# Where the softmax division of the second stack's attention is done: on the output, or on GpSimd ahead of the transposes

## The chip, the cores and the metric

The kernel runs on one core of a Trainium2 chip. A core has five engines with queues of their own: TensorE (PE; PEld is its weight load), VectorE (DVE), ScalarE (ACT), GpSimd (POOL) and SyncE (SP, here only DMA issue). They run side by side and are held together by semaphores alone. The metric is the device time of one execution in microseconds; below, "us" is that. The kernel before takes 3553.91 us, the median of 3 runs (3548.20 to 3556.32).

## The reference

Two transformer stacks of two layers each run one after the other on 512 positions of width 1024. The change touches only the attention of the second stack. There, 12 heads of 96 query/key and 64 value dimensions attend over 512 positions (plus 256 context positions as keys; in the first layer the 256 context positions are queries too, over themselves):

```python
def mla_attend(q_nope, q_rope, k_nope, k_rope, v):
    s = jnp.einsum('bqhd,bkhd->bhqk', q_nope, k_nope) + jnp.einsum('bqhr,bkr->bhqk', q_rope, k_rope)
    p = jax.nn.softmax(s.astype(jnp.float32) * SOFTMAX_SCALE, axis=-1).astype(v.dtype)
    return jnp.einsum('bhqk,bkhd->bqhd', p, v)
...
# in second_block, per layer:
att_l = blocked_attention(qn_l, qr_l, k_nope_all, k_rope_all, v_all)
four_l = fourier_mix(f_in, w_fourier[l], b_fourier[l])
mix_l = jnp.concatenate([four_l, att_l], axis=-1) @ w_out[l]
x = x + gt1 * mix_l
# then the gated feed-forward part; in layer 0 the same for the context
```

The division by the sum can be done on the probabilities p (128 queries x up to 768 keys, queries on the partitions) or after the product with v on the output (128 x 128, where the queries lie along the free axis).

## The kernel before, in words

Most of the time goes to large products, in which a weight slab (1 MB, 128 x 2048) is loaded by SP into one of two slots of `wst`, its upper part is cut off by ACT into `whi`, and the remainder `wst - whi` goes to `wlo`. For most slabs DVE computes the remainder, for 40 of them POOL (`split`, L684). Six of these 40 lie in the second stack, three for each layer's attention; ACT makes their `whi` in two halves (`next_group`, L1914) during pairs 0, 2 and 4.

The attention of the second stack is a hand-written software pipeline. The work is cut into **units**: one pair of heads for one block of 128 queries. Layer 0 has 6 pairs x 6 units (four units with 768 keys, then two with 256 keys, the context), layer 1 has 6 pairs x 4 units (768 keys); 60 units in all. In the text (l, p, n) is unit n of pair p in layer l. Each engine runs its own program over the units, written in this order for iteration u (`par` 0 and 1 are the two heads of the pair):

- PE: `logits(u+1, 0)` into PSUM; `turn(u, 0)`, four 128x128 transposes of the probabilities in `S2`; `logits(u+1, 1)`; `turn(u, 1)`; a "mid" projection for the next pair, if there is one; `turn(u, 2)`; `weighted(u-1)`, the product with the values, in PSUM bank 6; `denominators(u-1)`; an "end" projection, if there is one. The transposes share PSUM banks 4 and 5 in turn (`RING2`), projections of later pairs use bank 7.
- DVE: `maximum(u+1, 0)` (copies the logits from PSUM to `S2` and leaves the negated row maximum); `reciprocals(u)` of the two sums; `copy(u)`, the first transposed chunk to `PT2`; `maximum(u+1, 1)`; its share of the mid projection; `normalized(u-1)`, output times reciprocals; its share of the end projection.
- ACT: `exponential(u+1, 0)` in place in `S2`, with the row sum into `den2`; copy of chunk 1; mid projection; `exponential(u+1, 1)`; copy of chunk 2; `denominators(u-1)`; end projection.

The output lies with its queries along the free axis, so the reciprocals (one for each partition) have to be spread: PE's `denominators` (L1392) multiplies the broadcast reciprocals with the identity, ACT copies that to `Rs2` (L1942), and DVE multiplies (L2779). A pair's next projections stand at its first three units (`PROJECT_AT`): n = 0 K in mid and QA at the end, n = 1 KV and QB, n = 2 V and (layer 0) QC at the end. The later units of a pair, and all units of pair 5, carry none. PE's `weighted(u)` waits until `normalized(u-1)` has freed bank 6, and `maximum(u+1, par)` until the transposes of unit u-1 have freed `S2`.

Lines of the profile: L1348 logits, L1365 transposes, L1380 product with the values, L1392 spreading the reciprocals, L1316 to L1318 query projection, L2755 maximum, L2763 reciprocals, L2771 and L1934 copies of transposed chunks, L2779 normalisation, L1925 exponential (its second instruction, the accumulator read, delivers the sum), L1434 the first product after the attention.

Of the kernel before, what the change touches and what calls it, by code (L numbers as in the profile page):

```python
# [305 lines left out]
def turn_ring_2():  # L306

    at, copied, chunk, counts = {}, [], {}, {"ACT": 0, "DVE": 0}

    def place_(key, engine):  # L310
        at[key] = len(copied)
        counts[engine] += 1
        copied.append((engine, counts[engine]))

    for l in range(DEPTH):
        for u in range(len(UNITS2[l]) + 1):
            if u < len(UNITS2[l]):
                for c in range(blocks2(l, u) // 4):
                    chunk[l, u, c] = len(chunk)
                    place_(("T", l, u, c), "ACT" if c else "DVE")  # L320
            if u:
                place_(("R", l, u - 1), "ACT")
    return at, copied, chunk
# [57 lines left out]
def two_stacks(nc, io, out):  # L381
    m, s = Names(), Names()
    with ExitStack() as ctx:
# [110 lines left out]
        m.Rs2, at = place(nc, at, "Rs2", [P, 2, P])  # L494
# [110 lines left out]
        s.rden2_ready, s.o2_ready = sem("rden2_ready"), sem("o2_ready")  # L605

# [71 lines left out]
        @block.gpsimd  # L678
        def _(pool):
            def split(slab):  # L680

                pool.wait_ge(s.lo_ready, slab + 2)
                pool.wait_ge(s.hi_ready, slab + 3)
                nc.gpsimd.tensor_tensor(m.wlo[:, slab % 2, :], m.wst[:, slab % 2, :], m.whi[:, slab % 2, :].bitcast(F32),  # L684
                                        ALU.subtract).then_inc(s.lo_ready, 1)

            nc.gpsimd.memset(m.cs[:, :, :], 0.0).then_inc(s.cs_clear, 1)
            pool.drain()
            for l in range(DEPTH):
                for c in list(range(SL_A + 2, SL_ADA)) + [SL_MERGE, SL_MERGE + 1]:  # L690
                    if c != SL_B:
                        split(l * SLABS1 + c)
            for l in range(DEPTH):
                for c in (S2_HG + 2, S2_FOUR, S2_WOUT):
                    split(SLAB_BASE2 + l * SLABS2 + c)
            pool.drain()
# [3 lines left out]
        def _(pe):  # L700
# [512 lines left out]
            for l in range(DEPTH):  # L1213
# [144 lines left out]
                def turn(u, c):  # L1358

                    at = RING2["T", l, u, c]  # L1360
                    pe.wait_ge(s.exp2_ready, 2 * (unit0 + u + 1))
                    bank = ring_bank(at)
                    for b in range(4):
                        kb = 2 * c + b // 2
                        last = pe.transpose(ps[bank][:, b * P:(b + 1) * P],  # L1365
                                            m.S2[:, 2 * (u % 2) + b % 2, kb * P:(kb + 1) * P], ident)
                    last.then_inc(s.t2_done, 1)
# [18 lines left out]
                def denominators(u):  # L1386

                    pe.wait_ge(s.rden2_ready, unit0 + u + 1)
                    bank = ring_bank(RING2["R", l, u])
                    for par in range(2):  # L1390
                        c = 2 * (u % 4) + par
                        last = pe.matmul(ps[bank][VH * par:VH * (par + 1), 0:P],  # L1392
                                         m.rden2[:, c:c + 1].broadcast_to([P, VH]), ident, start=True, stop=True)
                    last.then_inc(s.t2_done, 1)

# [5 lines left out]
                for u in range(len(units) + 1):  # L1401
# [15 lines left out]
                    if u:  # L1417
                        weighted(u - 1)
                        denominators(u - 1)
                    if here["end"] is not None:  # L1420
                        project(p + 1, here["end"])
                copied2(pe, RING2["R", l, len(units) - 1])
# [131 lines left out]
        def _(act):  # L1554
# [261 lines left out]
            for l in range(DEPTH):  # L1816
# [101 lines left out]
                def exponential(u, par):  # L1918

                    w, unit = blocks2(l, u) // 2 * P, unit0 + u  # L1920
                    if unit >= 4:
                        act.wait_ge(s.rden2_ready, unit - 3)
# [12 lines left out]

                def denominators(u):

                    at, unit = RING2["R", l, u], unit0 + u
                    act.wait_ge(s.t2_done, at + 1)
                    if unit >= 2:  # L1940
                        act.wait_ge(s.o2_ready, unit - 1)
                    act.activation(m.Rs2[:, u % 2, :], ps[4 + at % 2][:, 0:P], ACT.Copy).then_inc(s.t2_act, 1)  # L1942
# [5 lines left out]
                for u in range(len(units) + 1):  # L1948
# [13 lines left out]
                    if u:  # L1962
                        denominators(u - 1)
# [85 lines left out]
        def _(dve):  # L2049
# [543 lines left out]
            for l in range(DEPTH):  # L2593
# [165 lines left out]
                def reciprocals(u):  # L2759

                    dve.wait_ge(s.exp2_ready, 2 * (unit0 + u + 1))
                    c = 2 * (u % 4)
                    nc.vector.reciprocal(m.rden2[:, c:c + 2], m.den2[:, c:c + 2]).then_inc(s.rden2_ready, 1)  # L2763
# [9 lines left out]
                def normalized(u):  # L2773
# [4 lines left out]
                    copied2(dve, RING2["R", l, u])  # L2778
                    TT(m.OT2[:, p, c0:c0 + P], ps[6][:, 0:P], m.Rs2[:, u % 2, :], ALU.mult).then_inc(s.o2_ready, 1)  # L2779
# [3 lines left out]
                for par in range(2):  # L2783
                    maximum(0, par)
                for u in range(len(units) + 1):
# [5 lines left out]
                    if u < len(units):  # L2791
                        reciprocals(u)
                        copy(u)
                    if u + 1 < len(units):
                        maximum(u + 1, 1)
                    if here["mid"] is not None:
                        projected(p + 1, here["mid"])
                    if u:
                        normalized(u - 1)
                    if here["end"] is not None:  # L2800
# [243 lines left out]
```

## Time and profile before

| what | value |
|---|---|
| median of 3 runs | 3553.91 us (3548.20 to 3556.32) |
| profiled execution | 3557.09 us, span 3555.3 us |
| PE busy / PEld busy | 3448.0 us (97%) / 2802.5 us (79%) |
| DVE busy | 2086.4 us (59%) |
| ACT busy | 1348.5 us (38%) |
| POOL busy | 187.9 us (5%), 45 instructions |
| chain that ended last | PE 83%, DVE 9%, ACT 4% |
| attention stretches of the second stack | about 1945 to 2174 and 2915 to 3100 us |

Times of the trace count from the start of the span. A timeline row gives the start and the duration of an instruction, or of several alike run together (x4), its engine and line, what it writes and reads, and in brackets how long the engine had been idle and what ended that. The busy figure of PE is modelled from pipelined instructions, so distances between starts of the weight loads (PEld) tell the pace more exactly.

### The profile page before, as it was taken

What the parts mean: (1) busy time and instruction counts of PE and PEld (TensorE: products, weight loads), DVE (VectorE), ACT (ScalarE), POOL (GpSimd) and SP (SyncE); (2) the same over time, 40 slices, a digit from 0 to 9 for tenths busy, and PEclk for the clock granted to TensorE, in tenths of its full rate; (3) what the DMA queues carried; (4) which work ended last, traced back from release to release, by engine and by line L of the source; (5) the groups of instructions that cost most, each with busy time, mean ns of one, the idle gap of its engine ahead of it and who ended that gap; (6) DMA issues with size and microseconds to landing.
All of it is one profiled execution on the core that took longest, in us unless ns stands there. A gap on an engine that the chain in (4) does not pass through costs nothing.

```text
span 3555.3 us, 53450 instructions
## 1 busy us (share of the span) xinstructions
PE 3448.0 (97%) x20094; PEld 2802.5 (79%) x20094; DVE 2086.4 (59%) x3313; ACT 1348.5 (38%) x2115; POOL 187.9 (5%) x45
## 2 busy tenths in 40 slices
PE   7999999999999999999998999999999989999998
PEld 6766888888777678888888776888888877688887
DVE  7876457444677745645566654653544665456546
ACT  5546333222453643322213554241323235534322
POOL 2321000000133010000000000000000001000000
PEclk9999999999999999999999999999999999999999
DMA  3235232222222633322221001111111110112222
GB/s 141 76 140 212 107 119 104 96 95 94 83 95 84 239 121 115 128 95 95 95 95 48 13 13 56 48 71 60 60 71 60 60 72 25 44 61 106 95 95 83
DMA packets 45639, 317.27 MB, mean 89 GB/s; under 512 B 4992, under 2 KB 7296, under 8 KB 8192
## 3 DMA queue, kind: packets, MB, share of 16 engines
q1 hardware_dynamic: 44720, 307.11, 23.4%
q10 hardware_dynamic: 720, 7.40, 0.5%
q8 instruction: 138, 2.26, 0.2%
q14 instruction: 61, 0.50, 0.0%
HBM read 312.39 MB, written 2.10 MB: 88 GB/s over the span
## 4 chain that ended last, share of the span: by engine, by line
PE 83%; DVE 9%; ACT 4%; DVEq 2%; issue 2%; POOL 0%; DMA 0%; ACTq 0%; SPq 0%; POOLq 0%
PE psum L722 21%; PE psum L726 21%; PE psum L723 21%; PE psum L1348 4%; PE psum L1380 2%; PE psum L1365 2%; DVE MA L2309 1%; PE psum L806 1%; PE psum L1183 1%; PE psum L1443 1%; PE psum L869 1%; ACT whi L1560 1%; ACT xs L1570 1%; PE psum L1316 1%; DVE BQK L2073 1%
## 5 line engine op out<-in xcount | busy, mean ns | idle before, releaser
L722 PE MATMUL psum<-xh,whi 128*128 128x512 f32 (+1 forms) x2224 | 857.6, 388 | 3.9 <-DVE xc L2064 2.1
L723 PE MATMUL psum<-xl,whi 128*128 128x512 f32 (+1 forms) x2224 | 850.9, 385 | 0.0
L1560 ACT ACTIVATE whi<-wst 128x2048 fp32r<-128x2048 f32 x234 | 447.0, 1910 | 582.9 <-PE psum L726 553.6
L2055 DVE TENSOR_TENSOR wlo<-wst,whi 128x2048 fp32r<-128x2048 f32 x200 | 458.2, 2291 | 176.8 <-ACT whi L1560 175.4
L726 PE MATMUL psum<-xh,wlo 128*128 128x512 f32 (+1 forms) x2224 | 536.5, 383 | 0.2
L722 PEld LDWEIGHTS psum<-xh,whi 128*128 128x128 f32 x2224 | 420.2, 189 | 97.3 <-issue 15.7
L723 PEld LDWEIGHTS psum<-xl,whi 128*128 128x128 f32 x2224 | 420.0, 189 | 82.4 <-issue 1.2
L726 PEld LDWEIGHTS psum<-xh,wlo 128*128 128x128 f32 x2224 | 409.7, 188 | 82.7 <-POOL wlo L684 1.1
L684 POOL TENSOR_TENSOR wlo<-wst,whi 128x2048 fp32r<-128x2048 f32 x40 | 187.2, 4680 | 2888.6 <-ACT whi L1914 1779.0
L722 PE MATMUL psum<-uh,whi 128*128 128x512 f32 x480 | 189.8, 395 | 0.0
L723 PE MATMUL psum<-ul,whi 128*128 128x512 f32 x480 | 189.5, 395 | 0.0
L722 PE MATMUL psum<-gh,whi 128*128 128x512 f32 (+1 forms) x576 | 188.3, 344 | 0.8 <-DVE gl L2906 0.8
L723 PE MATMUL psum<-gl,whi 128*128 128x512 f32 (+1 forms) x576 | 187.5, 343 | 0.0
L1348 PE MATMUL psum<-K,Q 96*128 96x256 f32 (+1 forms) x432 | 158.3, 486 | 1.4 <-DVE Q L2740 1.2
L1925 ACT ACTIVATE S<-S,nmax 128x768 f32<-128x768 f32 (+1 forms) x120 | 101.8, 848 | 127.2 <-DVE rden L2763 110.7
L1794 ACT ACTIVATE uh<-ur 128x512 f32 x64 | 40.5, 633 | 250.8 <-DVE ur L2553 250.8
L2573 DVE TENSOR_TENSOR hT<-hT,psum 128x512 f32<-128x512 f32 x64 | 44.0, 687 | 145.7 <-PE psum L726 126.3
L2839 DVE SCALAR_TENSOR_TENSOR hT<-psum,mod,hT 128x512 f32<-128x512 f32 (+1 forms) x80 | 51.3, 643 | 125.4 <-PE psum L726 125.4
L726 PE MATMUL psum<-uh,wlo 128*128 128x512 f32 x480 | 122.5, 395 | 0.0
L722 PE MATMUL psum<-xch,whi 128*128 128x256 f32 x488 | 121.3, 287 | 0.0
L722 PEld LDWEIGHTS psum<-gh,whi 128*128 128x128 f32 x576 | 109.4, 190 | 15.0 <-DVE gl L2906 1.2
L723 PE MATMUL psum<-xcl,whi 128*128 128x256 f32 x488 | 120.6, 286 | 0.0
(364 smaller groups left out, 5731.2 us busy)
## 6 DMA issues: line engine op xcount, KB each, us to landing
wst<-weights SPq DMA_DIRECT2D x288, 1024.0 KB, 4.8
dft<-c_dft ACTq DMA_DIRECT2D x2, 2688.0 KB, 10.5
hT<-x_t SPq DMA_DIRECT2D x4, 512.0 KB, 7.7
cT<-ctx_t ACTq DMA_DIRECT2D x1, 1024.0 KB, 6.9
out<-hT SPq DMA_DIRECT2D x1, 1024.0 KB, 5.4
out<-hT SPq DMA_DIRECT2D x2, 512.0 KB, 4.3
masks<-c_masks SPq DMA_DIRECT2D x1, 644.0 KB, 11.5
ropes<-c_ropes ACTq DMA_DIRECT2D x1, 512.0 KB, 7.6
```

Source lines behind the costliest of these rows:

```text
L684: nc.gpsimd.tensor_tensor(m.wlo[:, slab % 2, :], m.wst[:, slab % 2, :], m.whi[:, slab % 2, :].bitcast(F32), ALU.subtract).then_inc(s.lo_re ...
L722: pe.matmul(out, weights(m.whi, k), head(k), start=opens and n == 0, stop=False)
L723: pe.matmul(out, weights(m.whi, k), tail(k), start=False, stop=False)
L726: last = pe.matmul(out, weights(m.wlo, k), head(k), start=False, stop=closes and k == list(kts)[-1])
L1348: last = pe.matmul(ps[2 * par + c // 512][:, 0:w], m.Q4[0:QH, at, q0:q0 + P], m.K4[0:QH, at, side * T + c:side * T + c + w], start=True, s ...
L1365: last = pe.transpose(ps[bank][:, b * P:(b + 1) * P], m.S2[:, 2 * (u % 2) + b % 2, kb * P:(kb + 1) * P], ident)
L1380: mm = pe.matmul(ps[6][VH * par:VH * (par + 1), 0:P], m.V4[:, 4 * side + b // 2, col:col + VH], m.PT2[:, CHUNK2[l, u, c] % 5, (b % 4) * P: ...
L1560: act.activation(m.whi[:, slot, :], m.wst[:, slot, :], ACT.Copy).then_inc(s.hi_ready, 1)
L1925: act.activation(sc, sc, ACT.Exp, bias=m.nmax2[:, 2 * (u % 2) + par:2 * (u % 2) + par + 1], scale=-1.0, accum_out=m.den2[:, c:c + 1]).then ...
L2055: TT(m.wlo[:, slot, :], m.wst[:, slot, :], m.whi[:, slot, :].bitcast(F32), ALU.subtract).then_inc(s.lo_ready, 1)
L2573: TT(h, h, ps[(FR_MLP + j) % 4][:, :], ALU.add).then_inc(s.acc_free, 1)
L2839: STT(h, ps[t % 4][:, 0:n], g, h, ALU.mult, ALU.add).then_inc(s.acc_free, 1)
```

## The change

- `denominators` goes on both PE and ACT, with `Rs2` and the ring entries "R". The ring of PSUM banks 4 and 5 holds transposes alone.
- DVE's `reciprocals(u)` for both heads becomes `reciprocal(u, par)` for each. `reciprocal(u+1, 0)` stands after `copy(u)` and ahead of `maximum(u+1, 1)`; `reciprocal(u+1, 1)` stands after `normalized(u-1)`. For the first unit of a layer both stand ahead of the loop.
- POOL multiplies each head's probabilities in `S2`, in place, with the reciprocal, and signals `p2_normed`. PE's transposes wait for that instead of the exponential.
- DVE's `normalized` becomes a plain copy of bank 6.
- POOL's six weight remainders of the second stack (128x2048) are cut into four pieces of 128x512 each, one behind each of the first four units of pairs 1, 3 and 5.

```diff
+            def split_part(slab, n):
+                cols = slice(n * SLAB // 4, (n + 1) * SLAB // 4)
+                if n == 0:
+                    pool.wait_ge(s.lo_ready, slab + 2)
+                    pool.wait_ge(s.hi_ready, slab + 3)
+                ins = nc.gpsimd.tensor_tensor(m.wlo[:, slab % 2, cols], m.wst[:, slab % 2, cols],
+                                              m.whi[:, slab % 2, cols].bitcast(F32), ALU.subtract)
+                if n == 3:
+                    pool.drain()
+                    pool.sem_inc(s.lo_ready, 1)
+
             for l in range(DEPTH):
-                for c in (S2_HG + 2, S2_FOUR, S2_WOUT):
-                    split(SLAB_BASE2 + l * SLABS2 + c)
+                for u in range(len(UNITS2[l])):
+                    unit, w = UNIT2[l] + u, blocks2(l, u) // 2 * P
+                    for par in range(2):
+                        pool.wait_ge(s.rden2_ready, 2 * unit + par + 1)
+                        sc, c = m.S2[:, 2 * (u % 2) + par, 0:w], 2 * (u % 4) + par
+                        nc.gpsimd.tensor_scalar(sc, sc, m.rden2[:, c:c + 1], None, ALU.mult).then_inc(s.p2_normed, 1)
+                    p, n = divmod(u, len(SIDES2[l]))
+                    if p % 2 and n < 4:
+                        split_part(SLAB_BASE2 + l * SLABS2 + S2_HG + p // 2 + 2, n)
...
                 def turn(u, c):
-                    pe.wait_ge(s.exp2_ready, 2 * (unit0 + u + 1))
+                    pe.wait_ge(s.p2_normed, 2 * (unit0 + u + 1))
...
-                def denominators(u):
-
-                    pe.wait_ge(s.rden2_ready, unit0 + u + 1)
-                    bank = ring_bank(RING2["R", l, u])
-                    for par in range(2):
-                        c = 2 * (u % 4) + par
-                        last = pe.matmul(ps[bank][VH * par:VH * (par + 1), 0:P],
-                                         m.rden2[:, c:c + 1].broadcast_to([P, VH]), ident, start=True, stop=True)
-                    last.then_inc(s.t2_done, 1)
...
-                def reciprocals(u):
-
-                    dve.wait_ge(s.exp2_ready, 2 * (unit0 + u + 1))
-                    c = 2 * (u % 4)
-                    nc.vector.reciprocal(m.rden2[:, c:c + 2], m.den2[:, c:c + 2]).then_inc(s.rden2_ready, 1)
+                def reciprocal(u, par):
+
+                    dve.wait_ge(s.exp2_ready, 2 * (unit0 + u) + par + 1)
+                    c = 2 * (u % 4) + par
+                    nc.vector.reciprocal(m.rden2[:, c:c + 1], m.den2[:, c:c + 1]).then_inc(s.rden2_ready, 1)
...
-                    copied2(dve, RING2["R", l, u])
-                    TT(m.OT2[:, p, c0:c0 + P], ps[6][:, 0:P], m.Rs2[:, u % 2, :], ALU.mult).then_inc(s.o2_ready, 1)
+                    nc.vector.tensor_copy(m.OT2[:, p, c0:c0 + P], ps[6][:, 0:P]).then_inc(s.o2_ready, 1)
```

DVE's queue in the last pair of layer 1, before. ISA is the maximum with its accumulator read, `PT_138` the transposed chunk, `OT_126` the output, `Rs_139` the spread reciprocals:

```order
L2755 ISA S_137,nmax_144<-psum,none 128x768 [waits l2_done,t2_done]
L2755 ISA nmax_144 128x1
L2763 RECIPROCAL rden_143<-den_142 128x2 [waits exp2_ready]
L2771 COPY PT_138<-psum 128x512 [waits pv2_done,t2_done]
L2755 ISA S_137,nmax_144<-psum,none 128x768 [waits l2_done,t2_done]
L2755 ISA nmax_144 128x1
L2779 TENSOR_TENSOR OT_126<-psum,Rs_139 128x128 [waits t2_act,pv2_done]
```

The same stretch of DVE's queue in the changed kernel:

```order
L2749 ISA S_137,nmax_143<-psum,none 128x768 [waits l2_done,t2_done]
L2749 ISA nmax_143 128x1
L2765 COPY PT_138<-psum 128x512 [waits pv2_done,t2_done]
L2757 RECIPROCAL rden_142<-den_141 128x1 [waits exp2_ready]
L2749 ISA S_137,nmax_143<-psum,none 128x768 [waits l2_done,t2_done]
L2749 ISA nmax_143 128x1
L2772 COPY OT_126<-psum 128x128 [waits pv2_done]
L2757 RECIPROCAL rden_142<-den_141 128x1 [waits exp2_ready]
```

The second maximum now stands behind a reciprocal that waits for the first head's exponential of the same unit, and the second reciprocal stands behind the copy of the output, which waits for the product with the values.

PE's queue in the same pair, before, from the end of one unit's product with the values to the next unit's transposes (64x128 rows are halves of the output, 128x512 and 128x256 the logits):

```order
L1380 MATMUL psum<-PT_138,V_152 64x128 x3
L1392 MATMUL psum<-cst,rden_143 64x128 [waits t2_act,rden2_ready]
L1392 MATMUL psum<-cst,rden_143 64x128
L1348 MATMUL psum<-K_151,Q_150 128x512 [waits p2_act,p2_dve,max2_ready]
L1348 MATMUL psum<-K_151,Q_150 128x256
L1365 MATMUL psum<-cst,S_137 128x128 [waits t2_act,exp2_ready]
L1365 MATMUL psum<-cst,S_137 128x128 x3
```

And in the changed kernel:

```order
L1396 MATMUL psum<-PT_138,V_151 64x128 x3
L1364 MATMUL psum<-K_150,Q_149 128x512 [waits p2_act,p2_dve,max2_ready]
L1364 MATMUL psum<-K_150,Q_149 128x256
L1381 MATMUL psum<-cst,S_137 128x128 [waits t2_act,p2_normed]
L1381 MATMUL psum<-cst,S_137 128x128 x3
```

The two products with the reciprocals are gone, and the transposes wait for POOL's signal; nothing else in PE's order moves.

## Rows read from the trace of the kernel before

**Rows 1.** Windows, the two attention stretches: busy time and instructions of each engine, PEclk, DMA.

```profile
1945.00:2174.00 229.00, 222.48 (x1731) 168.93 (x1730) 130.01 (x312) 120.43 (x278) 13.57 (x3) 1.00 0.07 27
2915.00:3100.00 185.00, 180.66 (x1374) 136.32 (x1374) 99.15 (x214) 102.97 (x214) 13.67 (x3) 0.99 0.09 33
```

**Rows 2.** Timeline, second layer, one unit without projections, (1,5,1) to (1,5,2).

```profile
3077.95 0.58 PEld L1365 LDWEIGHTS psum<-cst,S 128*128 128x128 f32 x4
3078.47 0.96 DVE L2755 CUSTOM_DVE_ANT_0 S<-psum,none 128x768 f32<-128x768 f32 x1 [0.91 <-PE psum L1348]
3079.53 0.94 ACT L1925 ACTIVATE S<-S,nmax 128x768 f32<-128x768 f32 x1 [2.36 <-DVE rden L2763]
3080.20 0.96 DVE L2755 CUSTOM_DVE_ANT_0 S<-psum,none 128x768 f32<-128x768 f32 x1
3080.86 1.53 PE L1380 MATMUL psum<-PT,V 128*64 128x128 f32 x24
3082.11 0.19 ACT L1925 ACTIVATION_READ_ACCUMULATOR S<-S,nmax 128x1 f32 x1
3082.12 0.25 PEld L1392 LDWEIGHTS psum<-cst,rden 128*64 128x64 f32 x4
3082.54 0.30 PEld L1348 LDWEIGHTS psum<-K,Q 96*128 96x128 f32 x2 [0.17 <-issue]
3083.05 0.29 DVE L2779 TENSOR_TENSOR OT<-psum,Rs 128x128 f32<-128x128 f32 x1 [1.87 <-ACT Rs L1942]
3083.72 0.58 PEld L1365 LDWEIGHTS psum<-cst,S 128*128 128x128 f32 x4
```

**Rows 3.** Timeline, last short unit of a pair to the next pair's first, (0,3,5) to (0,4,0).

```profile
2101.49 0.58 PEld L1365 LDWEIGHTS psum<-cst,S 128*128 128x128 f32 x4
2102.02 0.96 DVE L2755 CUSTOM_DVE_ANT_0 S<-psum,none 128x768 f32<-128x768 f32 x1 [0.92 <-PE psum L1348]
2103.75 0.96 DVE L2755 CUSTOM_DVE_ANT_0 S<-psum,none 128x768 f32<-128x768 f32 x1
2105.65 0.19 ACT L1925 ACTIVATION_READ_ACCUMULATOR S<-S,nmax 128x1 f32 x1
2105.89 0.42 PEld L1365 LDWEIGHTS psum<-cst,S 128*128 128x128 f32 x4 [0.40 <-ACT S L1925]
```

**Rows 4.** Timeline of PE, layer 0, the end of the iteration before (0,4,4).

```profile
2134.27 0.39 PE L1380 MATMUL psum<-PT,V 128*64 128x128 f32 x4
2134.81 0.70 PE L1348 MATMUL psum<-K,Q 96*128 96x256 f32 x2
2135.34 0.60 PE L1365 MATMUL psum<-cst,S 128*128 128x128 f32 x4
```

**Rows 5.** Timeline, a unit reached behind two projections, (1,1,1).

```profile
2955.57 0.19 ACT L1925 ACTIVATION_READ_ACCUMULATOR S<-S,nmax 128x1 f32 x1
2959.53 0.58 PEld L1365 LDWEIGHTS psum<-cst,S 128*128 128x128 f32 x4
```

**Rows 6.** Groups of instructions: count, busy us, mean ns, idle before.

```profile
L684 POOL TENSOR_TENSOR wlo<-wst,whi 128x2048 fp32r<-128x2048 f32 x40 | 187.2, 4680 | 2888.6 <-ACT whi L1914 1779.0 <-ACT whi L1560 1109.2
L687 POOL MEMSET cs<- 128x512 f32 x1 | 0.5, 524 | 0.3 <-POOLq L3036 0.3
L1392 PEld LDWEIGHTS psum<-cst,rden 128*64 128x64 f32 x240 | 15.2, 137 | 0.0
L2763 DVE RECIPROCAL rden<-den 128x2 f32<-128x2 f32 x60 | 9.6, 159 | 0.0
```

**Rows 7.** Timeline, ACT's half of a weight slab and POOL's start behind it.

```profile
1981.63 1.05 ACT L1914 ACTIVATE whi<-wst 128x1024 fp32r<-128x1024 f32 x1
1982.82 4.52 POOL L684 TENSOR_TENSOR wlo<-wst,whi 128x2048 fp32r<-128x2048 f32 x1 [712.05 <-ACT whi L1914]
```

**Rows 8.** Timeline, the end of layer 1's attention.

```profile
3094.53 0.25 PEld L1392 LDWEIGHTS psum<-cst,rden 128*64 128x64 f32 x4
3095.45 0.29 DVE L2779 TENSOR_TENSOR OT<-psum,Rs 128x128 f32<-128x128 f32 x1 [2.23 <-ACT Rs L1942]
3095.81 0.73 PEld L1434 LDWEIGHTS psum<-dft,fT 128*128 128x128 f32 x4 [1.03 <-ACT Rs L1942]
```

**Rows 9.** Timeline, an idle time of PE with the clock kept.

```profile
1944.50 0.30 PE L1334 MATMUL psum<-whi,ckvh 128*128 128x128 f32 x1 [2.35 <-ACT K L1897]
```

More of the change, by code:

```diff
@@ L315, in turn_ring_2 @@
     for l in range(DEPTH):
[L316 to L322, printed above, removed]
+        for u in range(len(UNITS2[l])):
+            for c in range(blocks2(l, u) // 4):
+                chunk[l, u, c] = len(chunk)
+                place_(("T", l, u, c), "ACT" if c else "DVE")
     return at, copied, chunk
@@ L493, in two_stacks @@
         m.PT2, at = place(nc, at, "PT2", [P, 5, 4 * P])
-        m.Rs2, at = place(nc, at, "Rs2", [P, 2, P])
         m.none, at = place(nc, at, "none", [P, 1])
@@ L605, in two_stacks @@
         s.rden2_ready, s.o2_ready = sem("rden2_ready"), sem("o2_ready")
+        s.p2_normed = sem("p2_normed")
         s.oth_ready, s.mixed = sem("oth_ready"), sem("mixed")
@@ L692, in _ @@
                         split(l * SLABS1 + c)
-            for l in range(DEPTH):
-                for c in (S2_HG + 2, S2_FOUR, S2_WOUT):
-                    split(SLAB_BASE2 + l * SLABS2 + c)
+            def split_part(slab, n):
[8 more added lines that the diff above has]
+                    pool.sem_inc(s.lo_ready, 1)
+            for l in range(DEPTH):
+                for u in range(len(UNITS2[l])):
+                    unit, w = UNIT2[l] + u, blocks2(l, u) // 2 * P
[6 more added lines that the diff above has]
+                        split_part(SLAB_BASE2 + l * SLABS2 + S2_HG + p // 2 + 2, n)
             pool.drain()
@@ L1418, in _ @@
                         weighted(u - 1)
-                        denominators(u - 1)
                     if here["end"] is not None:
                         project(p + 1, here["end"])
-                copied2(pe, RING2["R", l, len(units) - 1])
                 pe.wait_ge(s.o2_ready, unit0 + len(units))
@@ L1921, in exponential @@
                     if unit >= 4:
-                        act.wait_ge(s.rden2_ready, unit - 3)
+                        act.wait_ge(s.p2_normed, 2 * (unit - 3))
                     act.wait_ge(s.max2_ready, 2 * unit + par + 1)
@@ L1934, in copy @@
                     act.activation(m.PT2[:, chunk % 5, :], ps[4 + at % 2][:, :], ACT.Copy).then_inc(s.t2_act, 1)
[L1936 to L1942, printed above, removed]
                 for n in range(len(PROJECTED[l])):
@@ L1961, in _ @@
                         copy(u, 2)
-                    if u:
-                        denominators(u - 1)
                     if here["end"] is not None:
@@ L2784, in _ @@
                     maximum(0, par)
+                for par in range(2):
+                    reciprocal(0, par)
                 for u in range(len(units) + 1):
@@ L2791, in _ @@
                     if u < len(units):
-                        reciprocals(u)
                         copy(u)
                     if u + 1 < len(units):
+                        reciprocal(u + 1, 0)
                         maximum(u + 1, 1)
@@ L2799, in _ @@
                         normalized(u - 1)
+                    if u + 1 < len(units):
+                        reciprocal(u + 1, 1)
                     if here["end"] is not None:
```

## The prediction

> **What bounds the kernel now.** I read the page first: PE is busy almost all the time, and the chain that ended last runs mostly through it. So a change counts if it takes work from PE or makes PE wait. The two stretches that the change touches come next [rows 1]: PE is busy for 222.5 of 229 us and 180.7 of 185 us, while DVE, ACT and POOL have room. POOL works for 13.6 us in each, three weight remainders. PE is the bound here, but only just: the softmax of a unit has to be done before PE comes to its transposes.
>
> So the third reading was the timeline, unit by unit. For each of the 60 units I compared the end of its second exponential with the start of the first transposes. The reader should see three kinds of unit. Behind a projection the probabilities are ready long before PE wants them: in (1,1,1) at 2955.76, and PE comes at 2959.53, 3.8 us later [rows 5]. Without projections 1.4 us are left: ready at 3082.30, wanted at 3083.72 [rows 2]. From a pair's last short unit to the next pair nothing is left: ready at 2105.84, PE starts at 2105.89 after an idle time of 0.40 us [rows 3]. The change puts two more steps between the exponential and the transposes, a reciprocal and a POOL instruction. What matters is in how many units they fit.
>
> **What goes.** The products with the reciprocals: 240 weight loads, 15.2 us busy [rows 6], so 0.25 us for each of 60 units. That is PE time, on the path wherever PE doesn't wait. ACT's copy to `Rs2` and the wait of DVE for it were hidden (1.87 us idle before the normalisation at 3083.05, and nobody waited for DVE there [rows 2]); their end only matters at a layer's end. The ring without its "R" entries lets a transpose wait for an earlier copy than before, worth nothing where the copies are in time.
>
> **What is added.** From the end of the second exponential to the transposes there was one wake-up, 0.05 us [rows 3]. Now: wake DVE 0.05, reciprocal 0.16 (159 ns for two sums, taken for one too [rows 6]), wake POOL 0.14 (ACT ends at 1982.68, POOL starts at 1982.82 [rows 7]), POOL's multiply T, wake PE 0.05. That is T + 0.40 us.
>
> T isn't in the trace. From below, a memset of 512 elements takes 524 ns, 1.02 ns an element, and only writes; the multiply also reads, so I don't go under 0.79 us for 768 elements and 0.26 for 256. From above, the remainder reads two tensors: 4.52 us for 2048 [rows 7], 2.21 ns an element, so 1.70 and 0.57 us. With one tensor read I stay nearer to the memset: 1.3 ns an element, T = 1.0 us, and 0.4 us for the short units.
>
> The Trainium skill (GPSIMD Engine Reference, Engine selection) advises against GpSimd for elementwise work, though it calls one-input operations roughly line-rate; the trace agrees with the two-input half of that, 4.52 us on POOL where the page gives 4497 ns. Its section Elementwise, side-by-side cycle accounting, has 769 ns for 512 elements in a tight loop. By that, as an estimate, T would be 1.15 us and the sum below 15 us; no row here shows it.
>
> Two orders on DVE cost more than the instructions. First, the second maximum now waits for the first head's exponential. In [rows 3] the first maximum starts at 2102.02. From the start of a maximum to the end of its exponential are 2.09 us (2103.75 to 2105.84). So that exponential ends at 2104.11, the reciprocal at 2104.32, and the second maximum starts there and not at 2103.75: 0.57 us later. Second, the second reciprocal stands behind the copy of the output, which waits for the product with the values.
>
> **The sum by kinds of transition**, from one unit's first transposes to the next unit's (58 of them):
>
> A. Last short unit to next pair, 5 times, layer 0. The exponential ends 0.57 later, at 2106.41; plus T + 0.40 gives 2107.81 against 2105.89. That is 1.92 each, 9.6 us.
>
> B. Full units without an end projection, 13 times. The product with the values ends at 3080.86 + 1.53 = 3082.39 [rows 2]. Then wake 0.05, copy 0.29 (as the normalisation), reciprocal 0.16, wake 0.14, T, wake 0.05: 3084.08 against 3083.72. The exponential would end at 3082.30 + 0.57 = 3082.87 in the first such unit, 0.14 behind the copy; once PE has waited, the first maximum starts earlier relative to PE and that goes. A group that waited runs through in 0.42 and not 0.58 us [rows 3], since its weight load no longer stands behind logits, which gives back 0.16. So 0.20 each, 2.6 us.
>
> C. Short logits in between, 6 times in layer 0. Product with the values ends at 2134.66 [rows 4]; plus 0.69 and 0.4 is 2135.75 against 2135.34, and 0.05 for the group's run: 0.45 each, 2.7 us.
>
> D. Four transitions in the last pairs, worked in the same way: 0.65 for (0,5,0) to (0,5,1), 1.07, 0.95, and 1.2 for the last of layer 1, where no logits follow the product. 3.9 us.
>
> E. The other 30, behind projections or with enough logits in between: all of it hides, and the 0.25 comes off. The slack is 3.8 us in [rows 5] against 0.6 + 1.4 + 0.25. Minus 7.5 us.
>
> F. Ends. A layer's first unit waits T + 0.35 more, 1.35 twice: 2.7 us. At a layer's end, before, the next product starts at 3095.81, behind products, ACT's copy and the normalisation [rows 8]; now the copy follows the product at once, 0.6 earlier, for each of the last two units: 4 x 0.6, minus 2.4 us.
>
> The quarters of weight remainders take about 1.15 us each (a quarter of 4.52) and start when PE starts transposing; POOL's next multiply comes over 2 us later, so they cost nothing. Without that cover a multiply would be late by what is left of a quarter. Their slabs are wanted two or more pairs later, or behind the Fourier part; SP's next load starts later by the time of the four units, and DMA's share in these stretches is 0.07 to 0.09 [rows 1].
>
> Sum: 9.6 + 2.6 + 2.7 + 3.9 - 7.5 + 2.7 - 2.4 = +11.6 us. The profiled execution took 3557.1 us, 3 us over the median of the runs; on the median the forecast is 3553.9 + 11.6 = 3565.5 us. T counts in 23 places in full and in 7 for the short units. At the lower bound the sum is 11.6 - 0.21 x 23 - 0.14 x 7 = +5.8, at the upper 11.6 + 0.70 x 23 + 0.17 x 7 = +28.9.
>
> **Rivals.**
> 1. POOL at the pace of the memset: 3553.9 + 5.8 = 3559.7 us, no change that can be told (about 0.2%, 7 us, is what a measurement tells here; that bound holds for the chances below). For it: only one tensor is read. Against it: a memset reads nothing.
> 2. POOL at the pace of the remainder: 3553.9 + 28.9 = 3582.8 us. For it: the only arithmetic that POOL shows runs so. Against it: half the reading.
> 3. Faster. PE hides the new steps nearly everywhere, because engines run ahead: when PE has waited once, the next unit's first maximum starts earlier relative to PE, so the order on DVE stops costing (0.57 of A goes too) and T is short. It needs T under 0.64 us, from where B turns into a gain (3083.08 + T against 3083.72). Then B to E give back up to 0.25 each: the full price is 15.2 + 2.4 = 17.6 us, 3536 us; with A still paid, 3545. Against it: the memset alone gives 0.79.
> 4. The clock. In A, PE idles for about 2.6 us five times. One idle time of 2.35 us [rows 9] lies at the edge of a stretch with PEclk 1.00 [rows 1], so I expect no fall. If each brought what layer 1's stretch lost (0.99 over 185 us, 1.9 us), 9 us more: 3575 us.
>
> **How the numbers follow.** Forecast 0.50 (own range 3561 to 3573), rival 1 0.20, rival 2 0.14, rival 3 0.09, rival 4 0.07. The range takes in rivals 1, 2 and 4 and the bounds of T, with 3 us for the spread of the runs: 3556 to 3584. Faster: rival 3, 0.08. Within 0.2%: rival 1 and the low edge of the forecast, 0.20. Slower: 0.72.
>
> **What would show it.** POOL's multiply has a row: its mean for 768 elements is T. PE's transposes should wait for POOL for about 2.6 us at 5 places in layer 0 and for about 0.5 us in units without projections; the stretch of layer 0 grows by about 10 us and that of layer 1 by about 1. Units behind projections should be 0.25 us shorter. The forecast is wrong if T is under 0.64 us, if DVE's second maximum doesn't start later in A, or if PE's clock falls in the idle times.

## The result and the profile after

The changed kernel takes 3620.43 us (median of 4 runs, 3617.52 to 3621.04) against 3553.94 us: a ratio of 1.0185, 95% interval 1.0172 to 1.0199. The forecast of 3565.5 us and its range up to 3584 are both missed; the direction was right. The profiled execution took 3617.5 us with a span of 3615.7 us. It was the shortest of the four, and that of the kernel before, 3557.1 us, was longer than the median: the two profiles are 60.4 us apart, the medians 66.5.

Groups of instructions on POOL between 1930 and 3200 us, one for each shape. These answer to [rows 6]:

```profile
L708 POOL TENSOR_SCALAR S<-S,rden 128x768 f32<-128x768 f32 x96 | 212.3, 2212 | 1584.3 <-DVE rden L2757 1583.8
L696 POOL TENSOR_TENSOR wlo<-wst,whi 128x512 fp32r<-128x512 f32 x24 | 30.6, 1275 | 0.0
L708 POOL TENSOR_SCALAR S<-S,rden 128x256 f32<-128x256 f32 x24 | 23.4, 975 | 31.8 <-DVE rden L2757 31.8
```

T is 2.21 us for 768 columns and 0.975 us for 256. The upper bound of the prediction, 1.70 and 0.57 us, was no bound.

The windows of the two stretches, [rows 1] before (columns: PE, PEld, DVE, ACT, POOL busy, then PEclk, DMA share, GB/s). The attention of layer 0 now runs on to about 2210, that of layer 1 from about 2957 to 3157:

```profile
1945.00:2174.00 229.00, 201.19 (x1355) 146.48 (x1353) 121.63 (x301) 95.58 (x202) 122.16 (x70) 0.93 0.03 10
2915.00:3100.00 185.00, 165.18 (x1095) 125.80 (x1096) 103.89 (x212) 83.40 (x156) 86.97 (x43) 0.96 0.10 34
```

PE is no longer busy throughout, and the granted clock has fallen from 1.00 to 0.93 in the first. The timeline of a full unit without projections, (1,5,0) to (1,5,1), for [rows 2]:

```profile
3127.99 0.42 PEld L1381 LDWEIGHTS psum<-cst,S 128*128 128x128 f32 x4 [1.70 <-POOL S L708]
3129.54 2.20 POOL L708 TENSOR_SCALAR S<-S,rden 128x768 f32<-128x768 f32 x1 [0.37 <-DVE rden L2757]
3130.09 0.96 DVE L2749 CUSTOM_DVE_ANT_0 S<-psum,none 128x768 f32<-128x768 f32 x1 [0.64 <-PE psum L1364]
3131.99 0.19 ACT L1929 ACTIVATION_READ_ACCUMULATOR S<-S,nmax 128x1 f32 x1
3132.35 0.29 DVE L2772 COPY OT<-psum 128x128 f32<-128x128 f32 x1 [1.30 <-PE psum L1396]
3132.56 0.15 DVE L2757 RECIPROCAL rden<-den 128x1 f32<-128x1 f32 x1
3132.80 2.20 POOL L708 TENSOR_SCALAR S<-S,rden 128x768 f32<-128x768 f32 x1 [1.06 <-DVE rden L2757]
3134.97 1.28 POOL L696 TENSOR_TENSOR wlo<-wst,whi 128x512 fp32r<-128x512 f32 x1
3135.06 0.42 PEld L1381 LDWEIGHTS psum<-cst,S 128*128 128x128 f32 x4 [1.70 <-POOL S L708]
```

The unit takes 7.07 us where it took 5.77. The order is as the prediction read it: copy of the output, reciprocal, multiply, transposes, each waiting for the one before. The quarter of a weight remainder (1.28 us) starts with the transposes and is done before the next multiply. From a short unit to the next pair, (0,3,5) to (0,4,0), for [rows 3]:

```profile
2125.59 0.42 PEld L1381 LDWEIGHTS psum<-cst,S 128*128 128x128 f32 x4 [0.42 <-POOL S L708]
2125.72 0.96 DVE L2749 CUSTOM_DVE_ANT_0 S<-psum,none 128x768 f32<-128x768 f32 x1 [1.20 <-PE psum L1364]
2127.96 0.96 DVE L2749 CUSTOM_DVE_ANT_0 S<-psum,none 128x768 f32<-128x768 f32 x1
2128.10 4.44 POOL L708 TENSOR_SCALAR S<-S,rden 128x768 f32<-128x768 f32 x2 [2.56 <-DVE rden L2757]
2129.86 0.19 ACT L1929 ACTIVATION_READ_ACCUMULATOR S<-S,nmax 128x1 f32 x1
2132.59 0.60 PEld L1381 LDWEIGHTS psum<-cst,S 128*128 128x128 f32 x4 [3.38 <-POOL S L708]
2133.39 2.77 PE L1364 MATMUL psum<-K,Q 96*128 96x512 f32 x4
```

7.00 us where it was 4.40. Here POOL itself is the chain: its two multiplies stand one behind the other (x2, 4.44 us). And behind this wait (3.38 us between weight loads, 2.98 us between PE's own products) PE runs at half speed: logits that take 1.46 us elsewhere take 2.77.

Two more rows answer to [rows 5] and [rows 8]. A unit behind two projections, (1,1,1), has its exponential ready 3.6 us early and doesn't wait:

```profile
3002.65 0.19 ACT L1929 ACTIVATION_READ_ACCUMULATOR S<-S,nmax 128x1 f32 x1
3006.40 0.58 PEld L1381 LDWEIGHTS psum<-cst,S 128*128 128x128 f32 x4
```

At the end of layer 1 the next product's weight load starts 0.66 us behind the last load of the values' product. Before, it was 1.28 us: the loads for the reciprocals, 0.25, and an idle time of 1.03 [rows 8].

```profile
3154.46 1.29 PEld L1396 LDWEIGHTS psum<-PT,V 128*64 128x64 f32 x24 [0.67 <-DVE OT L2772]
3156.07 0.29 DVE L2772 COPY OT<-psum 128x128 f32<-128x128 f32 x1 [1.66 <-PE psum L1396]
3156.41 0.73 PEld L1438 LDWEIGHTS psum<-dft,fT 128*128 128x128 f32 x4 [0.66 <-DVE OT L2772]
```

### The profile page after: what moved, and what is told of

It reads as the page before. It is cut to its first block, busy times and chain, and to the rows that moved or that the text cites. A ratio compares the mean times of both kernels' runs of the same rounds, so it can differ in the third digit from the quotient of the medians.

```text
span 3615.7 us, 52934 instructions
## 1 busy us (share of the span) xinstructions
PE 3458.5 (96%) x19854; PEld 2797.9 (77%) x19854; DVE 2099.6 (58%) x3373; ACT 1335.4 (37%) x2055; POOL 426.1 (12%) x183
## 3 DMA queue, kind: packets, MB, share of 16 engines
q8 instruction: 135, 2.21, 0.3%
## 4 chain that ended last, share of the span: by engine, by line
PE 80%; DVE 9%; ACT 4%; POOL 2%; issue 2%; DVEq 2%; DMA 0%; POOLq 0%; ACTq 0%; SPq 0%
PE psum L738 20%; PE psum L742 20%; PE psum L739 20%; PE psum L1364 3%; PE psum L1381 2%; POOL S L708 2%; PE psum L1396 2%; DVE MA L2303 1%; PE psum L822 1%; PE psum L1199 1%; PE psum L1447 1%; PE psum L885 1%; ACT whi L1564 1%; ACT xs L1574 1%; PE psum L1332 1%
## 5 line engine op out<-in xcount | busy, mean ns | idle before, releaser
L708 POOL TENSOR_SCALAR S<-S,rden 128x768 f32<-128x768 f32 (+1 forms) x120 | 235.7, 1964 | 1616.1 <-DVE rden L2757 1615.6
L681 POOL TENSOR_TENSOR wlo<-wst,whi 128x2048 fp32r<-128x2048 f32 x34 | 159.9, 4704 | 1107.6 <-ACT whi L1564 1107.3
L1364 PE MATMUL psum<-K,Q 96*128 96x256 f32 (+1 forms) x432 | 168.0, 511 | 1.2 <-DVE Q L2734 1.2
L1381 PE MATMUL psum<-cst,S 128*128 128x128 f32 x624 | 103.1, 295 | 58.5 <-POOL S L708 55.6
L1381 PEld LDWEIGHTS psum<-cst,S 128*128 128x128 f32 x624 | 78.8, 151 | 85.9 <-POOL S L708 71.5
L2749 DVE CUSTOM_DVE_ANT_0 S<-psum,none 128x768 f32<-128x768 f32 (+1 forms) x120 | 101.9, 849 | 51.0 <-PE psum L1364 49.9
L1364 PEld LDWEIGHTS psum<-K,Q 96*128 96x128 f32 x432 | 79.1, 201 | 59.5 <-issue 57.2
```

The source lines that it names most:

```text
L708: nc.gpsimd.tensor_scalar(sc, sc, m.rden2[:, c:c + 1], None, ALU.mult).then_inc(s.p2_normed, 1)
L1364: last = pe.matmul(ps[2 * par + c // 512][:, 0:w], m.Q4[0:QH, at, q0:q0 + P], m.K4[0:QH, at, side * T + c:side * T + c + w], start=True, s ...
L1381: last = pe.transpose(ps[bank][:, b * P:(b + 1) * P], m.S2[:, 2 * (u % 2) + b % 2, kb * P:(kb + 1) * P], ident)
L2749: nc.vector.tensor_tensor_reduce(m.S2[:, at, 0:w], psum[:, 1024 * par:1024 * par + w], m.none[:, 0:1].broadcast_to([P, w]), -1.0, -TAKEN, ...
```

## The experiments

Medians of before differ a little between the groups of runs (3552.7 to 3554.6 us); ratios are against those of the same group.

**The length of the multiply.** Two kernels change only the number of columns that it works on.

```diff
-   sc, c = m.S2[:, 2 * (u % 2) + par, 0:w], 2 * (u % 4) + par
+   sc, c = m.S2[:, 2 * (u % 2) + par, 0:64], 2 * (u % 4) + par        # e1_short
+   sc, c = m.S2[:, 2 * (u % 2) + par, 0:w // 2], 2 * (u % 4) + par    # e1_half
```

> The changed kernel with POOL's multiply cut to 64 columns a head (the rest of the probabilities is left undivided, so the output isn't the reference's); every wait and every order stays. Theory (the length of the multiply is what costs): the changed kernel shows 2.2 us for 768 columns and about 0.95 for 256, so some 0.5 us for 64. With T = 0.5 the prediction's own sum gives 11.6 - 0.5 x 23 + 0.1 x 7 = about +1 us against before, 3550 to 3560 us, and PE's clock doesn't fall in the attention. Rival (the extra hop and the order on DVE cost by themselves): at least 20 us over before, 3575 us or more.

Measured: 3558.15 us, ratio 1.0007 (0.9998 to 1.0016). The multiply took 460 ns. All hops, waits and orders of the change are in this kernel, and it costs 3.6 us by the medians, with an interval that takes in no change at all. The clock fell a little after all (0.98 and 0.99 in the two windows): three units behind a wait of PE took 1.6 to 1.7 us more than the same units of e5_warm below, in which PE keeps full speed there. The rival is out: of 66 us nearly all hangs on T, the waits and PE's slow stretches behind them together.

> The changed kernel with POOL's multiply over half the columns of each head (384 or 128; the other half is left undivided, so the output isn't the reference's). From the rows of 64, 256 and 768 columns (0.47, 0.975, 2.21 us) T should be about 1.3 and 0.65 us. Theory (time follows T): the prediction's sum with these gives 11.6 + 0.3 x 23 + 0.25 x 7 = +20 us, and less of the clock's fall than in the changed kernel: 3572 to 3590 us. Rival (a threshold, below which it is all hidden): 3560 us or less.

Measured: 3580.72 us, ratio 1.0066 (1.0046 to 1.0087), T = 1.25 us. The rival of a threshold is out too: 0.46, 1.25 and 2.21 us give +4, +26 and +66 us. The clock had already fallen here, to 0.94 and 0.96 in the two windows. A wait of PE for POOL, and the logits behind it, at (0,2,0):

```profile
2038.21 1.12 PE L1381 MATMUL psum<-cst,S 128*128 128x128 f32 x4 [2.34 <-POOL S L708]
2039.12 2.77 PE L1364 MATMUL psum<-K,Q 96*128 96x512 f32 x4
```

In six units (the first of each layer and of pairs 1 to 4 of layer 0) PE waited 2.3 to 2.6 us, and these took 1.6 to 2.9 us more than in e5_warm, 13.2 us together, half of the 26.

**What makes T.**

```diff
-   nc.gpsimd.tensor_scalar(sc, sc, m.rden2[:, c:c + 1], None, ALU.mult)
+   nc.gpsimd.tensor_scalar(sc, sc, 0.5, None, ALU.mult)                                       # e9_imm
+   nc.gpsimd.tensor_tensor(sc, sc, m.rden2[:, c:c + 1].broadcast_to([P, w]), ALU.mult)        # e10_tt
```

> The changed kernel with POOL multiplying by the constant 0.5 in place of the reciprocals (the output isn't the reference's). If the 2.21 us for 768 columns come from the multiplier that is read for each partition, the row should be clearly shorter, 1.0 to 1.5 us; if they are what this instruction costs on POOL whatever the multiplier, it stays at 2.2 us and the time at 3620 us.

> The changed kernel with POOL's multiply written as a product of two tensors, the second the reciprocal broadcast along the row. At the rate of the weight remainders (4.53 us for 2048 columns, 1.27 to 1.28 for 512, so 1.1 us for each 512 and 0.2 beside) 768 columns take about 1.8 us, 0.4 less than now: the two-input form would be the faster one, and the time falls by 0.4 x 23 = 9 us to about 3611 us. Rival (a two-input form is slower than one with a scalar, as the prediction took for granted): 3620 us or more.

POOL's rows of the two, e9_imm first:

```profile
L708 POOL TENSOR_SCALAR S<-S 128x768 f32<-128x768 f32 x96 | 205.2, 2138 | 1590.6 <-DVE rden L2757 1590.2
```

```profile
L708 POOL TENSOR_TENSOR S<-S,rden 128x768 f32<-128x768 f32 x96 | 141.5, 1475 | 1630.9 <-DVE rden L2757 1630.9
L708 POOL TENSOR_TENSOR S<-S,rden 128x256 f32<-128x256 f32 x24 | 16.0, 666 | 36.4 <-DVE rden L2757 36.4
```

With a constant it is 2.14 us, so the multiplier that is read for each partition isn't the reason (a single run: 3612.7 us). As a product of two tensors the same arithmetic takes 1.475 us, 3591.15 us in all, ratio 1.0105 (1.0088 to 1.0122): 29 us less than the changed kernel with one line written in another way. I had expected 9.

**The clock.**

```diff
+                def keep_busy(u):      # PE, called ahead of turn(u, 0)
+                    ...                # count: 8 at a layer's first unit, 6 or 3 in layer 0 as told below
+                    for _ in range(count):
+                        pe.matmul(ps[7][:, 0:256], ident, m.cst[:, 0:256], start=True, stop=True)
```

> The changed kernel with products of the identity with constants into PSUM bank 7 put ahead of those first transposes that wait longest for POOL (8 of 128x256 at each layer's first unit, 6 at the first unit of pairs 1 to 5 of layer 0, 3 at the other units of its pair 5; about 0.43 us each, so less than the wait they stand in). Nothing else is changed. Theory (PE's clock falls behind these idle times and its slow stretches are part of the cost): the granted clock of 1945 to 2174 rises from 0.93 to 0.98 or more and the time falls by 8 to 20 us, 3600 to 3612 us. Rival (the slow stretches lie in waiting anyway): 3617 to 3623 us.

Measured: 3602.77 us, ratio 1.0140 (1.0125 to 1.0156), 17.7 us under the changed kernel. T is unchanged at 2212 ns. The granted clock of layer 0 is back at 1.00 (the changed kernel has 0.93 and, from 2174 to 2220, 0.89), and behind the filled wait the logits take 1.46 us again:

```profile
1945.00:2174.00 229.00, 214.45 (x1488) 160.20 (x1489) 128.75 (x314) 103.32 (x217) 129.16 (x74) 1.00 0.05 18
2174.00:2220.00 46.00, 43.24 (x247) 26.59 (x245) 14.23 (x41) 15.55 (x39) 15.76 (x11) 1.00 0.16 62
```

```profile
2123.04 2.75 PE L1395 MATMUL psum<-cst 128*128 128x256 f32 x12
2126.18 0.66 PE L1381 MATMUL psum<-cst,S 128*128 128x128 f32 x4 [0.39 <-POOL S L708]
2126.68 1.46 PE L1364 MATMUL psum<-K,Q 96*128 96x512 f32 x4
```

The passage to the new pair still takes 7.00 us; what got shorter is the unit behind it, from 9.0 to 10.4 us to 7.3. So the slow stretches are a second cost that the waits bring with them, 17.7 of the 66.5 us.

**The order on DVE, alone and in company.** e3_order is the kernel before with the reciprocals at their new places; e8_maxfirst is the changed kernel with one pair of lines exchanged.

```diff
-                        reciprocals(u)          # e3_order, in the kernel before
                         copy(u)
                     if u + 1 < len(units):
+                        reciprocal(u + 1, 0)
                         maximum(u + 1, 1)
...
                         normalized(u - 1)
+                    if u + 1 < len(units):
+                        reciprocal(u + 1, 1)
...
-                        reciprocal(u + 1, 0)    # e8_maxfirst, in the changed kernel
                         maximum(u + 1, 1)
+                        reciprocal(u + 1, 0)
```

> The kernel before with nothing but the new places of the reciprocals on DVE: one for each head, the first ahead of the second maximum. Products with the reciprocals, ACT's copy and the whole weight remainders stay. The prediction's term: the second maximum 0.57 us later, paid at the 5 passages from a short unit to the next pair, +2.9 us, and 1 us for the rest: 3557 to 3559 us. Rival (the order holds up every unit without a projection too): +10 us or more.

> The changed kernel with DVE's second maximum ahead of the first head's reciprocal. Theory (POOL's two multiplies stand one behind the other and the first reciprocal starts that chain): the first multiply starts about 0.9 us later, the second with it, in all units in which PE waits for POOL, about 20 of them: 3632 to 3642 us. Rival (the later second maximum is what costs, as the prediction's term of 0.57 us says): 3608 to 3616 us.

e3_order: 3562.76 us, ratio 1.0022 (1.0012 to 1.0031), +8 us, twice what I gave it. The passages to the next pair cost 0.5 to 0.7 us each, 2.9 together, as reckoned (4.39 to 4.90 us in three of them). Two places had been put down as hidden. DVE's K copy stands behind the later second maximum, and PE needs it before the end projection: the first units of pairs 1 to 4 of layer 0 are 1.9 us longer together. And three transitions in the last pairs are 0.5 to 0.6 us longer each. In the profiles this makes 5.8 of the 8 us; the rest is not told apart. The K copy in unit (0,2,0), where PE waits 1.02 us in e3_order and 0.26 before:

```profile
2033.55 0.96 DVE L2755 CUSTOM_DVE_ANT_0 S<-psum,none 128x768 f32<-128x768 f32 x1
2034.55 0.69 DVE L2734 COPY K<-psum 64x512 f32<-64x512 f32 x1
2035.30 0.19 PEld L1316 LDWEIGHTS psum<-cqh,whi 128*128 128x128 f32 x1 [1.02 <-DVE K L2734]
```

e8_maxfirst: 3637.00 us, ratio 1.0234 (1.0218 to 1.0250). With a long T, putting the maximum ahead of the waiting reciprocal costs 17 us more, since POOL's chain of two multiplies starts with that reciprocal. Some of it is slow clock again: two units of layer 1 went from 8.19 to 9.9 us, with logits of 2.77 us. The reciprocal first is a loss without POOL's multiply and right with it.

**The quarters.**

```diff
-                    if p % 2 and n < 4:
-                        split_part(SLAB_BASE2 + l * SLABS2 + S2_HG + p // 2 + 2, n)
+                    if p % 2 and n == 0:
+                        split(SLAB_BASE2 + l * SLABS2 + S2_HG + p // 2 + 2)
```

> The changed kernel with POOL's weight remainders of the second stack whole again, 128x2048 in one piece behind the first unit of pairs 1, 3 and 5. Theory (a whole piece of 4.5 us stands ahead of the next unit's multiplies): it starts when PE starts transposing and ends at +4.6, the two multiplies of 2.2 us end at +9.0 where the second unit's transposes now come at +8.2 to +9.0, so up to 0.9 us six times: 3622 to 3626 us. Rival (POOL's queue has room for it, the quarters bring nothing): 3618 to 3621 us.

Measured: 3620.54 us, ratio 1.0189 (1.0173 to 1.0205), as the rival had it. Yet the mechanism of the theory is there: in layer 1 the units behind a whole piece take 8.89 us and not 8.19, and 8.87 and 8.74 in the last pair for 7.07; the layer is 5.2 us longer, 0.6 of it slow clock at its start. Layer 0 got 4.6 us shorter. 2.6 us of that lie in units in which PE's slow stretches fell differently, such as (0,5,3) to (0,5,4) with 5.13 for 6.39. Another 1.8 us lie in pair 1, where PE is at full speed in both kernels, and show a price of the quarters. The changed kernel there, then e6_whole:

```profile
2026.31 1.39 POOL L696 TENSOR_TENSOR wlo<-wst,whi 128x512 fp32r<-128x512 f32 x1
2026.43 1.82 DVE L2801 SCALAR_TENSOR_TENSOR hT<-hT,sm,r 128x512 f32<-128x512 f32 x1
2029.34 0.63 PE L1381 MATMUL psum<-cst,S 128*128 128x128 f32 x4 [1.42 <-DVE PT L2765]
```

```profile
2025.50 0.74 DVE L2801 SCALAR_TENSOR_TENSOR hT<-hT,sm,r 128x512 f32<-128x512 f32 x1
```

A DVE instruction of this stretch (an update of `hT` that has nothing to do with attention) takes 1.82 us beside a quarter and 0.74 without one; PE then waits 1.42 us for DVE's copy behind it, and 0.33 in e6_whole. So the quarters are worth some 4.5 us in layer 1 and cost 1.8 in layer 0; with the slow clock falling otherwise, the total shows neither.

**What could be won.**

```diff
-                    pe.wait_ge(s.p2_normed, 2 * (unit0 + u + 1))     # e2_nodiv; POOL's multiplies are left out
+                    pe.wait_ge(s.exp2_ready, 2 * (unit0 + u + 1))
...
+                def divided(u, par):      # e4_dve, on DVE behind maximum(u, 1) and the mid projection
+                    dve.wait_ge(s.exp2_ready, 2 * (unit0 + u) + par + 1)
...
+                    nc.vector.reciprocal(m.rden2[:, c:c + 1], m.den2[:, c:c + 1])
+                    dve.drain()
+                    TS(sc, sc, m.rden2[:, c:c + 1], None, ALU.mult).then_inc(s.p2_normed, 1)
```

> The changed kernel without any division (POOL's multiplies are left out, PE's transposes wait for the exponentials as before; the output isn't divided by the sums). It is the gain that the change could have at most. By the prediction's terms: 15.2 us of products on PE and 2.4 at the layers' ends, 3554 - 17.6 = 3536 us, plus 3 us for the order on DVE that stays = 3539. Rival (PE's saved time is taken back by waits for bank 7 and for the exponentials): 3548 us or more.

> The changed kernel with the multiply on DVE in place of POOL (reciprocal, drain, multiply in place, for each head behind the second maximum and the mid projection). If DVE needs 0.4 to 0.8 us for 768 columns (a DVE pass over 512 columns from PSUM takes 0.69 us in the trace, from SBUF it may be shorter), most units have the slack, DVE stays under 85% in the stretches, and PE keeps most of its 17.6 us: 3540 to 3548 us, faster than both kernels. Rival (DVE becomes the bound, since it is behind in the units with both a K copy and a rotation): 3554 to 3565 us.

e2_nodiv: 3542.03 us, ratio 0.9963 (0.9949 to 0.9976), 12.5 us less than before where I expected 15; e3_order shows that the order on DVE costs more than the 3 us taken for it. e4_dve: 3553.82 us, ratio 0.9998 (0.9989 to 1.0007), neither faster nor slower, where 3540 to 3548 us were expected. A multiply takes 0.62 us there, and layer 1 keeps its gain (5.55 for 5.77 us, 8.64 for 8.86, 6.87 for 7.09), but the passages in layer 0 pay it back (5.1 to 5.3 us for 4.40), and both layers start with a stretch of slow clock.

That led to e7_hybrid: the multiply on DVE where there is time, the old way where there is none.

```diff
+def is_spread(l, u):      # these units keep products, ring entry, Rs2 and normalisation of the kernel before
+    p, n = divmod(u, len(SIDES2[l]))
+    return n == 0 and (l == 0 or p == 0) or l == 0 and (n == 5 and p % 2 == 0 or p == 5 and n in (1, 3, 5)) or (l, p, n) == (1, 5, 3)
```

> A version meant to beat both. The multiply is on DVE (as in e4_dve) for the units that have time between exponential and transposes; the old way, products that spread the reciprocals and the transposes right behind the exponential, stays for 13 units: the first of each layer, the first of layer 0's later pairs, the last short ones of pairs 0, 2 and 4 and 4 in the last pairs. Against e4_dve (3554 us): 5 x 1.0 at the first units, 3 x 0.7 at the short ones, 3 at the starts of the layers, 1 in the last pairs: 3542 to 3546 us. Rival (mixing the two ways costs what it saves): 3552 us or more.

Measured: 3544.13 us, ratio 0.9970 (0.9959 to 0.9981). It beats both kernels, by 0.30% and by 2.1%. The passages are at 4.40 us again, the units behind them at 7.3 to 7.5. The old way stays for 14 of the 60 units (the expectation counts 13). Not all of the gain need be the division's: the first passage took 5.78 us in the kernel before, where DVE's update of `hT` took 2.67 us beside POOL's whole remainder. It takes 4.40 here, where POOL works in quarters and the update beside them takes 0.76. No run changes that alone.

## Why the prediction was wrong

Its frame held: which units have time, what follows what, and that the change makes the kernel slower. One term was mis-sized, T; one cost was put at nothing, the fall of PE's clock; and some waits that were put down as hidden were not.

**T, the step that failed.** "From above, the remainder reads two tensors: ... so 1.70 and 0.57 us." I took a two-input instruction for an upper bound of a one-input one. The scalar form costs 2.4 ns an element (2.21 and 0.975 us for 768 and 256) and even the product of tensors with a broadcast second input costs less. The Trainium skill calls one-input operations on GpSimd roughly line-rate (GPSIMD Engine Reference, Engine selection); neither this nor the 1.15 us estimated from its tight loop agrees with this trace, and the measurement decides. Its advice against elementwise work there is borne out: DVE needs 0.62 us for the same product. With the measured T the prediction's own sum is 11.6 + 1.21 x 23 + 0.575 x 7 = 43.5 us, beyond its range already. By kinds of transition, from the two profiles (the slow clock is what e5_warm takes off the same transitions):

| kind | forecast at T = 1.0 | the same at the measured T | measured | of which slow clock |
|---|---|---|---|---|
| A, 5 | +9.6 | +15.7 | +12.3 | |
| B, 13 | +2.6 | +18.3 | +17.7 | |
| C, 6 | +2.7 | +6.2 | +6.9 | 1.2 |
| D, 4 | +3.9 | +8.1 | +9.6 | 2.0 |
| E, 30 | -7.5 | -7.5 | +12.2 | 14.2 |
| F, starts and ends | +0.3 | +2.7 | +5.6 | 1.2 |
| sum | +11.6 | +43.5 | +64.3 | 18.6 |

B is the term that T carries: 1.30 us each in eight of the thirteen and 1.46 in the five behind a V projection, for which 0.20 + 1.21 = 1.41 follows from the forecast's working. A came out lower than 1.92 + 1.21 = 3.13 each: 2.6 to 3.0 in four of the five. In the rows of (0,3,5) DVE's second maximum did start 0.5 us later (2.24 us behind the first, 1.73 before), but it no longer counted: POOL's two multiplies in a row became the chain. The first passage grew by 1.4 us only, since it had been 5.78 us before, with PE waiting for a DVE that was held up beside POOL's whole remainder.

**Rival 4, the clock, given 0.07.** It happened, and not as a rival but on top: 17.7 us by the medians. The prediction judged from one idle time of 2.35 us without a fall and reckoned with 2.6 us of idling. With T = 2.21 PE itself waited 3.0 to 3.3 us at the passages and 4.3 at a layer's first unit, and behind these waits it ran at the lower of its two levels, 1.2 in place of 2.4 GHz. Nor would a shorter T have saved the step: in e1_half PE waited 2.3 to 2.6 us, as the prediction reckoned, and was slow behind all six of these waits. One idle time without a fall was no ground for expecting none. The slow clock is why E, "all of it hides", is at +12.2: it makes 14.2 us. Without them E is at -2.0.

**E, the rest.** Where nothing waited, the 0.25 us came off as forecast, or more (8.64 for 8.86 us in layer 1, 8.19 for 8.58). Not so at the fourth unit of layer 0's pairs, 8.54 for 8.37, where PE's weight load waited 0.43 us for POOL: with T = 1.25 it is 8.14. Nor between the two short units of a pair, 4.06 to 4.48 us for 4.04, which makes 2.2 us against the forecast. The units (0,1,1) and (0,1,2) add 1.3 us. e6_whole takes 0.7 off these two, and 1.1 off (0,1,3) in C, where DVE no longer stands beside a quarter: of the quarters, "they cost nothing" was wrong there.

**The order on DVE** was priced at 2.9 us, and at its place correctly; e3_order shows 8 by itself, since the K copy behind the maximum and the last pairs had been overlooked.

**F.** A layer's first unit waits 4.69 and 4.77 us and not 1.19 and 1.29: 3.5 more, not 1.35, being T and, again, two multiplies in a row. At a layer's end the step from the last values' product on gained 0.62 for the 0.6 us reckoned. From the last unit's transposes on, layer 0 gained 1.4 us, and layer 1 nothing (7.21 us for 7.15), as PE was slow there behind a wait of 2.8 us; e5_warm, with full speed, has 5.99.

The sum of it: 43.5 (own sum, measured T) + 18.6 (slow clock) = 62.1 of the 64.3 us that the two stretches are longer in the profiles. The last 2.2 us are misses that offset each other: without the slow clock A to D are 5.0 us under the sum at the measured T, E and F 7.2 over it. Outside the stretches the changed kernel's profile is 4 us shorter than the other, in work that the change doesn't touch; so the profiles as a whole are 60.4 us apart.

## What to carry to other kernels

A duration that the trace doesn't show is bounded only by the same instruction form on the same engine; another opcode on that engine, however similar, is a guess in both directions, and where 23 places hang on it, the range has to be as wide as that guess. When a pipeline gains a step, count the transitions that have less slack than the step, and then ask what the new idle times do to PE's clock, from more than one idle time in the trace. Ask also what runs on DVE while POOL works: moving or cutting a POOL instruction moves the DVE instructions that it delays. And look at each unit by itself: a step that doesn't fit everywhere may still pay where it does.

## What the runs showed of the hardware that was not expected

- POOL's forms of a multiply in place on 128x768 f32: by a scalar for each partition 2.21 us, by a constant 2.14 us, as two tensors with the second broadcast 1.475 us. By columns the scalar form took 0.46 (64), 0.655 (128), 0.975 (256), 1.25 (384) and 2.21 us (768).
- DVE's multiply in place, SBUF to SBUF, takes 0.62 us for 768 columns; its maximum over as many from PSUM takes 0.96 us. It and POOL get in each other's way: while POOL worked through four quarters in e7_hybrid, two such multiplies took 1.15 and 1.39 us (in the rows below), and POOL's quarters 5.29 us for four. So did DVE's update of `hT`, which reads two tensors from SBUF: 0.74 us alone, 1.82 beside a quarter in the changed kernel, 2.67 beside a whole remainder in the kernel before (the last row, behind POOL's in [rows 7]).

```profile
3059.28 0.62 DVE L2795 TENSOR_SCALAR S<-S,rden 128x768 f32<-128x768 f32 x1
3060.57 5.29 POOL L706 TENSOR_TENSOR wlo<-wst,whi 128x512 fp32r<-128x512 f32 x4 [53.86 <-ACT whi L1937]
3063.58 1.15 DVE L2795 TENSOR_SCALAR S<-S,rden 128x768 f32<-128x768 f32 x1
3064.88 1.39 DVE L2795 TENSOR_SCALAR S<-S,rden 128x768 f32<-128x768 f32 x1
```

```profile
1985.22 2.67 DVE L2804 SCALAR_TENSOR_TENSOR hT<-hT,sm,r 128x512 f32<-128x512 f32 x1
```

- The Trainium skill (SBUF — State Buffer, Who interferes with whom) says that DVE in a 2-port mode and GpSimd block each other for a whole instruction. The rows of DVE's multiply agree in kind; which of DVE's instructions were in such a mode, no run here shows.
- PE's slow stretches behind waits for POOL: in the changed kernel logits took 2.77 us for 1.46 behind a wait of 2.98 us, in e1_half behind one of 2.34. In e1_short two waits of 1.70 us came out differently: 2.76 us for the logits behind one, at (0,1,0), and 1.46 behind the other, at (0,2,0). The length of the wait alone doesn't decide it.
